# Gated recurrence of a two-layer trunk: five decay levels and blocks of four in two visits of TensorE, on 32-column tiles

## The reference, cut to what matters

```python
bcum = jnp.cumsum(gc, axis=2)                       # log decay, summed
diff = bcum[:, :, :, None, :] - bcum[:, :, None, :, :]
attn = jnp.sum(qc[:, :, :, None, :] * kc[:, :, None, :, :] * exp(diff), axis=-1)   # t >= s
o = attn @ v + (qc * exp(bcum)) @ state
```

## Time and profile before

| | |
|---|---|
| median of 3 runs | 1025.34 us |
| the profiled execution | 1027.41 us |
| its span, first to last instruction | 1025.6 us |
| TensorE (PE) busy | 1013.7 us, 99% |
| DVE, ACT, POOL busy | 642.7, 517.2, 287.4 us |
| share of the chain that ended last | PE 92%, DVE 5% |
| granted TensorE clock, mean | 0.997 |

### The profile page before, as it was taken

The page is one execution under the profiler, slowest core; times in us unless marked ns, Lnnn a source line. Parts: engine busy times, 40 slices in busy tenths (PEclk is TensorE's granted clock), DMA queues, the critical chain, the costliest instruction groups (busy, mean ns, idle before and its releaser), DMA issues.

```text
span 1025.6 us, 15346 instructions
## 1 busy us (share of the span) xinstructions
PE 1013.7 (99%) x6406; PEld 855.2 (83%) x6406; DVE 642.7 (63%) x840; ACT 517.2 (50%) x804; POOL 287.4 (28%) x144
## 2 busy tenths in 40 slices
PE   8999999999999999999999999999999999999997
PEld 7878999788888888888888989988888888888876
DVE  6978965899444443536638689479973444444552
ACT  6866665865633222323366766567546323232333
POOL 1122114324332323324112111153243232322430
PEclk9999999999999999999999999999999999999999
DMA  7532122122232323325243222212232232322602
GB/s 222 153 103 64 63 83 83 42 83 83 62 103 83 103 82 103 99 68 162 83 134 103 67 79 84 83 49 77 83 103 62 82 103 84 101 89 96 204 2 82
DMA packets 93428, 94.71 MB, mean 92 GB/s; under 512 B 2272, under 2 KB 91568, under 8 KB 93360
## 3 DMA queue, kind: packets, MB, share of 16 engines
q1 hardware_dynamic: 93232, 93.70, 29.8%
q10 hardware_dynamic: 128, 0.04, 0.0%
HBM read 91.64 MB, written 2.10 MB: 91 GB/s over the span
## 4 chain that ended last, share of the span: by engine, by line
PE 92%; DVE 5%; ACT 1%; issue 1%; DMA 1%; SPq 0%; DVEq 0%; ACTq 0%
PE pj L512 27%; PE pj L513 26%; PE pj L514 26%; PE mx L649 2%; PE mx L512 1%; PE mx L513 1%; PE mx L514 1%; PE mx L612 1%; PE mx L709 1%; PE mx L677 1%; PE mx L597 1%; PE mx L687 1%; PE mx L589 1%; DMA x_tokens<-in_x 1%; DVE rope_cos L1427 1%
## 5 line engine op out<-in xcount | busy, mean ns | idle before, releaser
L1168 POOL TENSOR_TENSOR w_lo<-w_raw,w_hi 128x1024 fp32r<-128x1024 f32 (+1 forms) x89 | 195.9, 2201 | 566.5 <-ACT w_hi L825 566.3
L512 PE MATMUL pj<-h_hi,w_hi 128*128 128x512 f32 x832 | 329.7, 396 | 0.4 <-DVE w_lo L1278 0.4
L514 PE MATMUL pj<-h_hi,w_lo 128*128 128x512 f32 x832 | 324.2, 390 | 0.0
L513 PE MATMUL pj<-h_lo,w_hi 128*128 128x512 f32 x832 | 324.1, 389 | 0.0
L825 ACT ACTIVATE w_hi<-w_raw 128x1024 fp32r<-128x1024 f32 (+1 forms) x179 | 159.1, 938 | 160.3 <-PE pj L514 160.1
L1278 DVE TENSOR_TENSOR w_lo<-w_raw,w_hi 128x1024 fp32r<-128x1024 f32 (+1 forms) x90 | 159.9, 1777 | 67.9 <-ACT w_hi L825 67.7
L512 PEld LDWEIGHTS pj<-h_hi,w_hi 128*128 128x128 f32 x832 | 156.2, 188 | 34.8 <-issue 3.2
L514 PEld LDWEIGHTS pj<-h_hi,w_lo 128*128 128x128 f32 x832 | 156.2, 188 | 33.1
L513 PEld LDWEIGHTS pj<-h_lo,w_hi 128*128 128x128 f32 x832 | 156.3, 188 | 31.9 <-issue 1.0
L1392 DVE TENSOR_TENSOR merge_gate<-pj,rstd 128x512 f32<-128x512 f32 x48 | 33.2, 692 | 162.9 <-PE pj L514 162.9
L943 ACT ACTIVATE merge_gate<-merge_gate,small 128x512 f32<-128x512 f32 x48 | 34.3, 715 | 89.3 <-DVE merge_gate L1392 89.3
(11 more groups left out here) (259 smaller groups left out, 1502.0 us busy)
## 6 DMA issues: line engine op xcount, KB each, us to landing
w_raw<-in_w_in SPq DMA_DIRECT2D x61, 1024.0 KB, 5.5
w_raw<-in_w_branch SPq DMA_DIRECT2D x24, 512.0 KB, 3.4
w_raw<-in_w_out SPq DMA_DIRECT2D x6, 1024.0 KB, 5.2
x_tokens<-in_x SPq DMA_DIRECT2D x4, 512.0 KB, 7.3
w_raw_last<-in_w_out SPq DMA_DIRECT2D x2, 1024.0 KB, 8.1
sp_w_rows<-in_sp_w SPq DMA_DIRECT2D x2, 512.0 KB, 6.3
out<-out_low SPq DMA_DIRECT2D x4, 256.0 KB, 2.0
out<-out_high SPq DMA_DIRECT2D x4, 256.0 KB, 2.3
```

The source lines that it names most:

```text
L512: pe.matmul(bank, wh, ah, start=first, stop=False)
L513: pe.matmul(bank, wh, al, start=False, stop=False)
L514: return pe.matmul(bank, wl, ah, start=False, stop=final)
L1168: return pool.tensor_tensor(out=dst, in0=full, in1=hi.bitcast(f32), op=ALU.subtract)
```

## The change

There are now 5 levels (64, 32, 16, 8, 4 tokens), and the pairs inside a block of four tokens are one step: both k and q are scaled by exp of plus or minus half of (2 bcum - b1 - b2), with b1 and b2 the sums at the block's two middle tokens, and one matmul and one mask give all pairs t >= s of the block, the diagonal among them. DIAG becomes (12, 26). The visits are two: blocks of four, levels 0 and 1 in hook d+1, and levels 2, 3, 4 in hook d+4. The late steps are in hooks d+9 to d+12 for p = 0 (as before) and d+7 to d+10 for p = 1 (33 to 36 instead of 34 to 37). Blocks and levels 1 to 4 use stationary tiles of 32 columns that go round the four 32-column groups of the array.

```diff
-LEVELS = 7
-DIAG = (12, 25)
-PAIRS = ((0,), (1, 2), (3, 4), (5, 6))
+LEVELS = 5
+DIAG = (12, 26)
+LATE = (9, 7)
+MASKS = 4 * (LEVELS + 1)
+VISITS = ((0, 1), (2, 3, 4))
...
                     for hb in range(2 * TB):
-                        hh, tb = divmod(hb, TB)
-                        for half in range(2):
-                            rows = slice(half * 64, half * 64 + 64)
-                            b = slice(tb * P + half * 64, tb * P + half * 64 + 64)
-                            last = pe.matmul(M[4][rows, hb * 64:(hb + 1) * 64], KK[p][:, hh, b], QC[p][:, hh, b],
+                        for g in range(4):
+                            b = slice(hb * P + g * 32, hb * P + (g + 1) * 32)
+                            last = pe.matmul(M[4][g * 32:(g + 1) * 32, hb * 32:(hb + 1) * 32], HK[p][:, b], HQ[p][:, b],
                                              start=True, stop=True)
...
                     for hb in range(2 * TB):
-                        for half in range(2):
-                            blk = ops[:, hb * P + half * 64:hb * P + half * 64 + 64]
+                        for g in range(4):
+                            blk = ops[:, hb * P + g * 32:hb * P + (g + 1) * 32]
                             upper = blk.rearrange("p (b u s) -> p b u s", u=2, s=s)[:, :, 1, :]
-                            last = pe.matmul(bank[half * 64:half * 64 + 64, hb * 32:(hb + 1) * 32], blk, upper,
+                            last = pe.matmul(bank[g * 32:(g + 1) * 32, hb * 16:(hb + 1) * 16], blk, upper,
                                              start=True, stop=True)
...
-                    for i, levels in enumerate(PAIRS):
+                    for i, levels in enumerate(VISITS):
                         for lev in levels:
-                            hooks[d + 1 + 2 * i].append((level, p, lev))
+                            hooks[d + 1 + 3 * i].append((level, p, lev))
                     for step, f in enumerate((transpose_khat, state_updates, recurrent_out, head_norm)):
-                        hooks[d + 2 + LEVELS + step].append((f, p))
+                        hooks[d + LATE[p] + step].append((f, p))
...
+                def block4_exp(p):
+                    act.wait_ge(diff_done, upto(diff_done, (LEVELS + 2) * p + 1))
+                    act.activation(E[1][:, :], E[0][:, :], ACT.Exp, scale=0.5)
+                    act.activation(E[0][:, :], E[0][:, :], ACT.Exp, scale=-0.5).then_inc(decay_ready, 1)
...
+                    phase[d - 2].append((block4_exp, p))
+                    for lev in range(LEVELS):
+                        phase[d + (-1, -1, 0, 0, 3)[lev]].append((decay_exp, p, lev))
...
+                    b = BC[p][:, :, :].rearrange("p h t -> p (h t)").rearrange("p (b u) -> p b u", u=4)
+                    mid2 = E[1][:, 0:2 * T // 4]
+                    chained(dve.tensor_tensor(out=mid2, in0=b[:, :, 1], in1=b[:, :, 2], op=ALU.add))
+                    dve.scalar_tensor_tensor(out=E[0][:, :].rearrange("p (b u) -> p b u", u=4), in0=b, scalar=2.0,
+                                             in1=mid2.unsqueeze(2).to_broadcast([P, 2 * T // 4, 4]),
+                                             op0=ALU.mult, op1=ALU.subtract).then_inc(diff_done, 1)
...
+                    dve.tensor_tensor(out=HK[p][:, :], in0=KK[p][:, :, :].rearrange("p h t -> p (h t)"),
+                                      in1=E[0][:, :], op=ALU.mult)
+                    evacuated(dve, FIRST[("cq", p)] + 1, layer)
+                    dve.tensor_tensor(out=HQ[p][:, :], in0=QC[p][:, :, :].rearrange("p h t -> p (h t)"),
+                                      in1=E[1][:, :], op=ALU.mult).then_inc(ops_ready, 1)
...
+                    chained(dve.memset(AT[:, :, :], 0.0))
+                    for g in range(4):
+                        rows = slice(g * 32, (g + 1) * 32)
+                        last = dve.copy_predicated(at4[rows, :, g * 32:(g + 1) * 32],
+                                                   MASK4[rows, :].unsqueeze(1).to_broadcast([32, 2 * TB, 32]),
+                                                   M[4][rows, 0:T // 2].rearrange("p (b t) -> p b t", t=32))
```

More of the change, by code:

```diff
@@ L79, in constants @@
 def constants():
-    c = np.zeros((P, P + 8 * LEVELS + 8), np.float32)
-    masks = c[:, P:P + 8 * LEVELS].view(np.uint8)
+    c = np.zeros((P, P + MASKS + 8), np.float32)
+    masks = c[:, P:P + MASKS].view(np.uint8)
     c[:, 0:P] = np.eye(P)
-    for lev in range(1, LEVELS):
+    for i in range(P):
+        for t in range(i % 32, i % 32 // 4 * 4 + 4):
+            masks[i, t] = 1
+    for lev in range(2, LEVELS):
         s = 64 >> lev
@@ L1529, in take_diagonal @@
                     at4 = AT[:, :, :].rearrange("p h (b t) -> p (h b) t", t=P)
-                    dve.memset(at4[64:128, :, 0:64], 0.0)
-                    for half in range(2):
-                        rows = slice(half * 64, half * 64 + 64)
-                        last = dve.tensor_tensor(out=at4[rows, :, half * 64:half * 64 + 64],
-                                                 in0=M[4][rows, :].rearrange("p (b t) -> p b t", t=64),
-                                                 in1=ID[rows, rows].unsqueeze(1).to_broadcast([64, 2 * TB, 64]),
-                                                 op=ALU.mult)
+                    chained(dve.memset(AT[:, :, :], 0.0))
[4 more added lines that the diff above has]
+                                                   M[4][rows, 0:T // 2].rearrange("p (b t) -> p b t", t=32))
                     last.then_inc(at_evac, 1)
@@ L1716, in program @@
-                    for i in (1, 2):
-                        for lev in PAIRS[i + 1]:
-                            phase[d + 1 + 2 * i].append((diffs, p, lev))
-                        for lev in PAIRS[i]:
-                            phase[d + 2 + 2 * i].append((take_level, p, lev))
-                        for lev in PAIRS[i + 1]:
-                            phase[d + 2 + 2 * i].append((operands, p, lev))
-                    phase[d + LEVELS].append((block_diffs, p))
-                    for lev in PAIRS[3]:
-                        phase[d + LEVELS + 1].append((take_level, p, lev))
@@ L1726, in program @@
-                    phase[d + LEVELS + 1].append((decayed, p))
-                    phase[d + LEVELS + 4].append((states, p))
-                    phase[d + LEVELS + 6].append((head_scaled, p))
+                    phase[d - 2].append((block4_diffs, p))
+                    phase[d - 1].append((block4_operands, p))
+                    for lev in (0, 1):
+                        phase[d - 1].append((diffs, p, lev))
+                    for lev in (0, 1):
+                        phase[d].append((operands, p, lev))
@@ new lines, in program @@
+                    for lev in (2, 3):
+                        phase[d].append((diffs, p, lev))
+                    phase[d + 2].append((take_block4, p))
+                    for lev in (0, 1):
+                        phase[d + 2].append((take_level, p, lev))
+                    for lev in (2, 3):
+                        phase[d + 3].append((operands, p, lev))
+                    phase[d + 3].append((diffs, p, 4))
+                    phase[d + 4].append((operands, p, 4))
+                    for lev in (2, 3, 4):
+                        phase[d + 5].append((take_level, p, lev))
@@ L1729, in program @@
+                    phase[d + 5].append((block_diffs, p))
+                    phase[d + 6].append((decayed, p))
+                    phase[d + LATE[p] + 2].append((states, p))
+                    phase[d + LATE[p] + 4].append((head_scaled, p))
                 for j in range(4):
```

131 lines of the change are left out of this document (74 added, 57 removed).

## The result

The kernel after takes 1034.65 us (1030.36 to 1035.34, 4 runs) against 1025.34 (4 runs). The ratio is 1.0081, with a 95% interval of 1.0068 to 1.0094. It is slower; the prediction was 1019.0, faster, with a range that ended at 1031. The four executions of the kernel after differ in their mean granted clock: 1030.36 us had 0.994, the other three, 1034.58 to 1035.34, had 0.989 to 0.991.

The account below looks back on a forecast made before the run. TensorE, busy 99% of the span, was taken as the bound. Its work fell by 17.5 us and stalls added 11.2, so -6.3 us: 1021.1 for the profiled execution, 1019.0 for the median, range 1009 to 1031.

Parts of the forecast that it names:

- TensorE's work, -17.5: TensorE over the whole kernel: records -16.9, fewer visits -2.6, changes of tile shape +2.0 us.
- The record of 8 ns: Each 32-column record on TensorE was taken to cost 8 ns, with the four column groups running side by side.
- 1.5 to 1.7 were to be the sign: Sign of being right: the hook 30 visit of 192 records lasts 1.5 to 1.7 us; 3 us or more is wrong.
- two groups: Rival: only two column groups work at a time, 16 ns a record, 9.2 us more, 1028.2 us; chance 0.13.
- issue at 19 ns: Rival: TensorE can't start records closer than 19 ns on average, 13.0 us on top, 1032.0 us; chance 0.17.
- The rule of a least distance of 25 ns: Skill's claim that matmul starts never come closer than about 25 ns; estimated from it: 288 records cost 7.2 us, time 1038.6.
- Stalls from late semaphores, 8.8 without level 4: TensorE's waits for late ACT and DVE work: 3.1 and 0.3 in hook 13's two layers, 5.4 at job 28.
- before attend: TensorE waits for ACT's late copy of the transposed probabilities, at about 99 us in layer 0; sign: idle 2 to 4 us.
- before the transposes: Hook 13, layer 0: DVE normalises the probabilities at 93.0 where TensorE wanted them at 92.65, 0.4 us late.
- job 28: Projection job, both layers: DVE's half of the weights of unit 14 comes late; stall 2.7 us in each layer, 5.4 together.
- Level 4, 2.4: Level 4 operands wanted in the hook that makes them: tie for p = 0, 1.2 us a layer for p = 1.
- A microsecond waited is a microsecond lost: Unwritten step in the sum: the stalls, 11.2 us in all, are each added to the time at their length.

Follow-up runs that it names:

- j: g with one order changed: on DVE the level 4 operands are made ahead of the copies of levels 2 and 3; 1016.32 us.
- run 27: Not a label of a run: the words say that TensorE had already executed 27 records of level 4 in hook 16.
- e3: Kernel after, with matmuls of ones (13 in layer 0, 5 in layer 1) filling TensorE's wait before attend; 1025.76 us.
- k: i with one order changed: level 4 operands made ahead of the copies of levels 2 and 3; 1018.72 us.
- i: The spread schedule of g, with 64-column tiles instead of 32-column ones; 1022.2 us.
- m: j with levels 2 and 3 in hook 30 worked out four times over into the same place; 1039.11 us, one execution.
- e1: Kernel after, with ACT's exps of levels 2 and 3 one phase later, behind the copy of the transposed probabilities; 1024.12 us.
- e4: Kernel after, with 32 tiny matmuls (64 records, 128 instructions) added at the start; 1035.69 us.
- g: Kernel after with its work spread over the phases, each operand made a phase or more ahead of use, narrow tiles; 1027.72 us.
- h: Kernel after, schedule unchanged, with blocks and levels 1 to 4 on 64-column tiles on two column groups; 1029.28 us.
- e2: e1 with DVE's differences of levels 2 and 3 also one phase later; 1025.4 us.

## Why the prediction was wrong

*TensorE's work, -17.5.* Right to 1 us. The balance gives -16.7. The record of 8 ns measured 9.0 to 9.8 in hook 30 (1.73 and 1.88 us for the visit, for which 1.5 to 1.7 were to be the sign) and 8.6 in the level 4 visit of j; the four column groups do run at once, which put an end to the rivals "two groups" and "issue at 19 ns". The rule of a least distance of 25 ns that the prediction quoted from the Trainium skill ("TensorE: Matmul & The Clock Gate", "Wait — 56ns, not 53.3ns?") doesn't hold across column groups: 192 records in 1.88 us. The estimate that the prediction made from it, 2.1 us more for TensorE than before, is off with it.

*Stalls from late semaphores, 8.8 without level 4.* Right, place by place: before attend 3.1 and 1.1 against 2.7 and 0.3, before the transposes 0.5 more than before against 0.4, job 28 2.5 and 2.5 against 2.7 and 2.7. Sum 9.7. The count of DVE's queue, operation by operation, was good to about 1 us over 20.

*Level 4, 2.4.* Wrong in its mechanism and in its place. The forecast had 1.2 in each layer in hook 30 and a tie in hook 16. In hook 30 nothing was waited for; in hook 16 the profile has 2.38 and 2.35, and there the operands were ready (DVE done at 127.82, and TensorE had run 27 records of level 4). That 2.4 stands in both is chance. These were instruction supply; with the third stall they are 7.6, where 2.4 stood for another cause. That is 5.2 us missing.

*A microsecond waited is a microsecond lost.* This is the step that failed, and it was never written down as a step: the sum adds each stall at its length. The profile of before had no wait of more than 1.5 us after the start, and its clock was 1.00 from 11.8 us until the last matmuls, so I put in no price. But its start had one: a wait of 2.3 us for the tokens, with 3.4 us at 0.50 from 8.4 on. The runs: 9.0 us, the largest part of the error. That the waiting does it is shown by e3 for the first and longest stretch, where a filled wait of the same length keeps the clock at 1.00; for the other four it rests on their places, behind a wait or a stall each time, and on j, k and i, which have no wait over 1.4 us and no such stretch. The Trainium skill describes it ("TensorE: Matmul & The Clock Gate", "HAM oscillation — how this bites in real kernels"): a kernel that waits for DMA comes back each time at the lower clock. Here the waits were for a semaphore or for instructions, and the lower clock came behind five of the six of 2 us and more. The prediction named three waits of over 2 us and should have asked this of each.

*Sum.* Forecast -6.3 on the profiled execution; add 9.0 for the clock, 5.2 for supply, 0.9 for the sizes of the waits, 0.8 on TensorE, less 2.3 at the start: +7.3, as measured. (TensorE's part is what was left over, so the sum has to close; that it comes within 1 us of the forecast is the test.)

*The range and the chances.* The rivals for slower were both about the rate of TensorE. "Issue" had the right place (a dense visit is held back by its instructions) and the wrong law: not 19 ns on each record, but 8 to 10 ns and then 1.8 to 2.7 us at a block border (m), and none at all in most visits. That its 1032.0 lies near 1034.65 is chance. No rival dealt with what a wait does afterwards.

What stays open: which wait is followed by half clock. The profiles of the kernel after, e1 to e4, g and h have 22 waits of 2.0 us or more behind the start, and 18 were followed by it; four were not (2.35 in the kernel after, 2.53 in e1, 2.02 in e2 and in e3). Below 2.0 it came behind 1.86 and 1.95 in e4 and behind two of 1.6, 5.6 us apart, in e1, and not behind 1.84, 1.84 and 1.80 in h. Open too is what makes an instruction packet late where weights are being moved, and how far j could still fall: its 5 us of waits more than k's were not pursued.

## What to carry to other kernels

When TensorE is the bound and a change lets others come late, price each new TensorE wait of 2 us or more at its length and then, most of the time (18 of 22 here), 1.6 to 3.2 us of half clock behind it, and look at the granted clock before believing a sum of waits; to keep it at work, or to change the order on a strict queue so that what TensorE wants comes first, can be worth more than the matmuls saved (18.3 us here for the same records, 11.4 of them by one swap). Small tiles are paid in instructions: count the instructions of a visit and how long 256 of them last, and break up a run in which that is shorter than a fetch. A new schedule is not judged by its time alone but by its largest wait: g looked like a refutation, and was two lines from the best kernel.

## What was not expected of the hardware

- Instruction supply stalls TensorE in dense runs: 1.8 to 2.7 us at every 128 narrow records in m, with a 16 KB packet at each, and none in the same visit with wide tiles at 29 ns a record.
- A wait for a semaphore ahead of a dense stretch, with weights being moved, can bring such a stall too: 2.85 us in the kernel after, gone in e1 with the same instructions on TensorE.
- A pause of 2.0 to 3.1 us is mostly followed (18 of 22) by 3.4 us, once 6.8 us, at 0.50 of the clock, while TensorE is fully busy again (3.40 busy of 3.40).
- Tiles of 32 columns on four column groups go at 8.6 to 9.8 ns a record, two records to a matmul.
- A few unrelated instructions at the start (e4) move the stalls to other places and change their sum (5.2 us, where it was 7.6), with no change in the work.
